# Gathers of u and v in turn, with single-buffer releases and early row numbers

## The reference

```python
cand = (v1[..., :, None] + v2[..., None, :]).reshape(bsz, seq, PEER_HEADS, PEER_TOPK * PEER_TOPK)
sc, ci = lax.top_k(cand, PEER_TOPK)
experts = (jnp.take_along_axis(i1, ci // PEER_TOPK, axis=-1) * PEER_NKEYS
           + jnp.take_along_axis(i2, ci % PEER_TOPK, axis=-1))
gates = jax.nn.softmax(sc, axis=-1)

def peer_block(args):
    hb, eb, gb = args
    u_sel = jnp.take(peer_u, eb, axis=0)
    z = jnp.einsum('td,tkd->tk', hb, u_sel)
    act = jax.nn.gelu(z, approximate=False) * gb
    return jnp.einsum('tk,tkd->td', act, jnp.take(peer_v, eb, axis=0))
```

## Time and profile before

| | |
|---|---|
| Time, median of 3 runs | 1563.23 us (1555.8 to 1563.44) |
| Profiled execution: span from first to last instruction | 1523.7 us; the time around the span was not recorded for it |
| PE, DVE, ACT, POOL busy | 1222.4, 989.9, 438.1, 645.2 us |
| Gather queue (q0) | 268.47 MB, 47.5% of 16 engines' span |
| Mean granted TensorE clock | 0.888 of 2.4 GHz |

### The profile page before, as it was taken

The page is one execution under the profiler, slowest core; times in us unless marked ns, Lnnn a source line. Parts: engine busy times, 40 slices in busy tenths (PEclk is TensorE's granted clock), DMA queues, the critical chain, the costliest instruction groups (busy, mean ns, idle before and its releaser), DMA issues.

```text
span 1523.7 us, 15861 instructions
## 1 busy us (share of the span) xinstructions
PE 1222.4 (80%) x5450; PEld 813.5 (53%) x5450; DVE 989.9 (65%) x1812; ACT 438.1 (29%) x853; POOL 645.2 (42%) x641
## 2 busy tenths in 40 slices
PE   6997898998888576675788768667667988799998
PEld 2983778566563222232344323223225977599986
DVE  6699879575555656756677555675446666478773
ACT  1564312122122112121131211212115452365651
POOL 4164203007564777767776777677750020000000
PEclk9998799999998887888999778788878999799999
DMA  9354031438998999999999999999986423355540
GB/s 355 134 193 140 27 111 56 166 111 313 356 385 316 351 352 340 355 354 358 368 338 335 358 345 357 339 366 368 345 290 234 157 93 111 124 166 166 175 165 28
DMA packets 139764, 380.97 MB, mean 250 GB/s; under 512 B 10707, under 2 KB 37742, under 8 KB 139706
## 3 DMA queue, kind: packets, MB, share of 16 engines
q0 software_dynamic: 73728, 268.47, 47.5%
q1 hardware_dynamic: 64656, 108.87, 20.7%
q10 hardware_dynamic: 1322, 2.85, 0.6%
HBM read 379.10 MB, written 1.05 MB: 249 GB/s over the span
## 4 chain that ended last, share of the span: by engine, by line
PE 56%; POOL 13%; DVE 13%; issue 8%; DMA 6%; ACT 3%; SPq 0%; POOLq 0%; DVEq 0%; ACTq 0%
PE banks L1048 20%; POOL arena L655 7%; PE banks L757 7%; PE banks L759 7%; PE banks L758 7%; POOL arena L647 6%; DMA arena<-in_peer_u,arena 4%; PE banks L1016 3%; DVE arena L1912 2%; DVE weight_ring L1836 2%; PE banks L701 2%; DMA weight_ring<-in_cond_w 1%; PE banks L997 1%; PE banks L730 1%; ACT arena L1540 1%
## 5 line engine op out<-in xcount | busy, mean ns | idle before, releaser
L1048 PE MATMUL banks<-arena 128*128 128x512 f32 x1012 | 508.9, 667 | 206.3 <-ACT arena L1540 182.3
L1048 PEld LDWEIGHTS banks<-arena 128*128 128x128 f32 x1012 | 214.8, 216 | 497.7 <-issue 286.9
L2169 DVE SCALAR_TENSOR_TENSOR arena<-arena 128x1024 f32<-128x1024 f32 x256 | 312.5, 1226 | 237.6 <-DMA arena<-in_peer_u,arena 231.8
L655 POOL DMA_INDIRECT arena<-in_peer_v,arena x256 | 271.2, 1059 | 142.1 <-issue 73.1
L647 POOL DMA_INDIRECT arena<-in_peer_u,arena x256 | 271.2, 1059 | 96.8 <-issue 69.7
L759 PE MATMUL banks<-hi_h,low_slot 128*128 128x256 f32 (+2 forms) x600 | 172.5, 288 | 0.0
L1533 ACT ACTIVATE arena<-arena 128x8 f32<-128x8 f32 x32 | 6.7, 208 | 455.6 <-DVE arena L2169 455.6
L759 PEld LDWEIGHTS banks<-hi_h,low_slot 128*128 128x128 f32 (+2 forms) x600 | 114.0, 190 | 0.6
L757 PE MATMUL banks<-hi_h,hi_w 128*128 128x256 f32 (+1 forms) x352 | 101.3, 288 | 2.7 <-DVE lo_h L2270 2.7
L758 PE MATMUL banks<-lo_h,hi_w 128*128 128x256 f32 (+1 forms) x352 | 100.0, 284 | 0.0
L1540 ACT ACTIVATE arena<-ident,arena 128x128 f32<-128x128 f32 x256 | 78.2, 388 | 13.4 <-DVE arena L2173 12.9
(11 more groups left out here) (367 smaller groups left out, 2070.6 us busy)
## 6 DMA issues: line engine op xcount, KB each, us to landing
weight_ring<-in_cond_w SPq DMA_DIRECT2D x12, 2048.0 KB, 9.6
weight_ring<-in_w_in SPq DMA_DIRECT2D x11, 2048.0 KB, 8.2
weight_ring<-in_ffn_w_up SPq DMA_DIRECT2D x20, 1024.0 KB, 6.8
weight_ring<-in_ffn_w_down SPq DMA_DIRECT2D x5, 2048.0 KB, 7.7
weight_ring<-in_w_out SPq DMA_DIRECT2D x4, 2048.0 KB, 7.7
weight_ring<-in_peer_wq SPq DMA_DIRECT2D x4, 2048.0 KB, 12.6
arena<-in_peer_u,arena POOLq DMA_INDIRECT x256, 5.9
arena<-in_peer_v,arena POOLq DMA_INDIRECT x256, 6.1
```

What stands on the lines that cost most here:

```text
L655: g.indirect_dma_start(v_rows[:, j, :], None, A["peer_v"], bass.IndirectOffsetOnAxis(ap=stage[:, r, j:j + 1], axis=0)).then_inc(sem(f"v_in ...
L1048: last = mm(acc[i], diag[:, r, j, :], v_rows[:, j, i * 512:(i + 1) * 512], start=False, stop=False)
L2169: ins = v.scalar_tensor_tensor(out=u_rows[:, j, :], in0=u_rows[:, j, :], scalar=1.0, in1=h2[:, t, :], op0=ALU.mult, op1=ALU.mult, accum_ou ...
```

## The change

Releases by the buffer: PE adds one to `v_free` behind each buffer and not behind the eighth, and DVE adds one to `u_free` with each dot. ACT's waits are for the same events with the new counts. POOL copies the 16 row numbers of a head at once, into one of three places of `stage`, in the first round of the head before, behind v gather 6. The gathers of u and v alternate: u of the next round, v of this round, each behind its own release. There is no loop; all 512 gathers are written out.

```diff
-            def gather(n):
-                for r in range(2):
...
-                    for j in range(8):
-                        g.indirect_dma_start(u_rows[:, j, :], None, A["peer_u"],
...
+            def copy_rows(n):
+
+                pool.wait_ge(sem("experts_ready"), n + 1)
+                g.tensor_copy(stage[:, n % 3, :], experts[:, n * TOPK:(n + 1) * TOPK]).then_inc(sem("staged"), 1)
+
+            rounds = 2 * (LAST + 1)
...
+            def gather_u(rnd, j):
+
+                if rnd:
+                    pool.wait_ge(sem("u_free"), (rnd - 1) * 8 + j + 1)
+                g.indirect_dma_start(u_rows[:, j, :], None, A["peer_u"], row_of(rnd, j)).then_inc(sem(f"u_in_{j}"), 16)
...
+                if rnd:
+                    pool.wait_ge(sem("v_free"), (rnd - 1) * 8 + j + 1)
...
+            copy_rows(0)
+            pool.wait_ge(sem("staged"), 1)
+            for j in range(8):
+                gather_u(0, j)
+
+            for rnd in range(rounds):
+                for j in range(8):
+                    if rnd + 1 < rounds:
+                        if rnd % 2 and j == 0:
+                            pool.wait_ge(sem("staged"), (rnd + 1) // 2 + 1)
+                        gather_u(rnd + 1, j)
+                    gather_v(rnd, j)
+                    if rnd % 2 == 0 and j == 6 and rnd // 2 < LAST:
+                        copy_rows(rnd // 2 + 1)
@@ sum_v (PE)
-                    last.then_inc(sem("v_free"), 1)
+                        last.then_inc(sem("v_free"), 1)
@@ activate (ACT)
-                    act.wait_ge(sem("u_free"), n * 2 + (r + 1))
+                    act.wait_ge(sem("u_free"), n * 16 + 8 * (r + 1))
...
-                        act.wait_ge(sem("v_free"), n * 2 + (r - 1))
+                        act.wait_ge(sem("v_free"), n * 16 + 8 * (r - 1))
@@ dots (DVE)
-                        ins.then_inc(sem("u_free" if j == 7 else "u_part"), 1)
+                        ins.then_inc(sem("u_free"), 1)
```

More of the change, by code:

```diff
@@ L373, in block_kernel @@
         aw = at(SM + 272, 2, 8)
-        stage = at(SM + 288, 16).bitcast(U32).rearrange("p (a b) -> p a b", b=8)
+        stage = at(SM + 864, 3 * TOPK).bitcast(U32).rearrange("p (a b) -> p a b", b=TOPK)
         experts = at(SM + 304, (NT * PEER_H + 1) * TOPK).bitcast(U32)
@@ L631, in _ @@
                            sem("off_ready"))
-            def gather(n):
-                for r in range(2):
-                    pool.wait_ge(sem("experts_ready"), n + 1)
-                    g.tensor_copy(stage[:, r, :], experts[:, bass.ds(n * TOPK + 8 * r, 8)]).then_inc(sem("staged"), 1)
-                    pool.wait_ge(sem("staged"), n * 2 + (r + 1))
-                    g.nop(nofuse=True)
-                    first = isinstance(n, int) and n * 2 + r == 0
-                    if not first:
-                        pool.wait_ge(sem("u_free"), n * 2 + r)
-                        g.nop(nofuse=True)
-                    for j in range(8):
-                        g.indirect_dma_start(u_rows[:, j, :], None, A["peer_u"],
-                                             bass.IndirectOffsetOnAxis(ap=stage[:, r, j:j + 1], axis=0)
-                                             ).then_inc(sem(f"u_in_{j}"), 16)
-                    if not first:
-                        pool.wait_ge(sem("v_free"), n * 2 + r)
-                        g.nop(nofuse=True)
-                    for j in range(8):
-                        g.indirect_dma_start(v_rows[:, j, :], None, A["peer_v"],
-                                             bass.IndirectOffsetOnAxis(ap=stage[:, r, j:j + 1], axis=0)
-                                             ).then_inc(sem(f"v_in_{j}"), 16)
@@ L659, in _, with row_of @@
-            gather(0)
-            gather(1)
-            for t in range(NT):
-                with pool.Fori(max(2, t * PEER_H), (t + 1) * PEER_H) as n:
-                    gather(n)
+            def copy_rows(n):
+                pool.wait_ge(sem("experts_ready"), n + 1)
+                g.tensor_copy(stage[:, n % 3, :], experts[:, n * TOPK:(n + 1) * TOPK]).then_inc(sem("staged"), 1)
+            rounds = 2 * (LAST + 1)
+            def row_of(rnd, j):
+                return bass.IndirectOffsetOnAxis(ap=stage[:, rnd // 2 % 3, 8 * (rnd % 2) + j:8 * (rnd % 2) + j + 1], axis=0)
@@ new lines, in gather_u, with gather_v @@
+            def gather_u(rnd, j):
+                if rnd:
+                    pool.wait_ge(sem("u_free"), (rnd - 1) * 8 + j + 1)
+                g.indirect_dma_start(u_rows[:, j, :], None, A["peer_u"], row_of(rnd, j)).then_inc(sem(f"u_in_{j}"), 16)
+            def gather_v(rnd, j):
+                if rnd:
+                    pool.wait_ge(sem("v_free"), (rnd - 1) * 8 + j + 1)
+                g.indirect_dma_start(v_rows[:, j, :], None, A["peer_v"], row_of(rnd, j)).then_inc(sem(f"v_in_{j}"), 16)
```

## The result

The changed kernel took 1600.99 us (median of 4 runs, 1589.13 to 1604.01), the kernel before 1559.51 on the same chip (1553.23 to 1563.44): ratio 1.0277 [1.0196, 1.0358]. I had forecast 1530. The runs behind it fell on several chips, and that matters here: on most of them before takes 1531 to 1532 us, and there the change is 0.995 to 0.996. On one more, where before takes 1555.6, it is 1.019. I call the two kinds the fast and the slow chips; each chip was measured in one session, so its own speed and what ran beside it then can't be told apart. Each run is compared with before on its own chip. The interval of the first result lies wholly above 1, so the change was slower there, by about 2 to 3.6%.

The account below looks back on a forecast made before the run. POOL, with 38 + 22 us of waits in the 619.5 us middle stretch, and DMA at 0.95 were the near limits. Middle 29, start 2 and end 2 us less: span 1523.7 to 1491, plus 39.5 gives 1530 us; range 1513 to 1562.

Parts of the forecast that it names:

- Part 4: POOL's new pace in the middle stretch: 391 us of gathers, 52 of lengthening beside dots, 127 gaps, 3 copies: 573 us.
- The rule that I weighed: Two-input DVE instructions and GpSimd SBUF reads exclude each other: up to 1.23 us a dot; judged too large against the trace.
- Part 3: Row numbers copied once a head on POOL: 21.7 us of waits and 2.7 of copies go; slack 1 to 3 us.
- The start: 344.8 to 487.7 us: sum 0 ends 4 to 5 us later, then regained; net 2 us less.
- Part 1: Single-buffer releases: each gather waits for its own dot or sum; no instruction added on DVE and PE, nothing lost on ACT.
- Part 2: POOL's u and v in turn: slack 15 us for v, 5 for u; POOL's 37.9 us of waits for PE go.
- Part 5: DMA in the middle stretch: the same packets take 590 us at a full share, which can be had.
- Part 6: POOL's unrolled program: at most a few hundred KB more instructions to load, beside 218 MB of rows; costs nothing.
- The wait's price: Rival: a wait on each POOL gather costs time, deciding above 0.11 us each; slower, chance 0.11.
- DMA's limit: Rival: DMA gives no more than now, 353 GB/s in the middle, about 1560 us; chance 0.13, of which 0.09 no change.
- PE's clock: Rival: PE's short steps keep it at 1.2 GHz, 27.9 us a round, +106 us; chance 0.04.
- The copy stall: Rival: with later landings POOL stops at the copy, losing 20 of the 29 us, about 1550; chance 0.11.

Follow-up runs that it names:

- e4: The changed kernel on a fast chip, against the kernel before: 1524.99 us, ratio 0.9959.
- the first run: The changed kernel's first measurement and profile, on a slow chip, against the kernel before: 1600.99 us, ratio 1.0277.
- e8: The changed kernel with dots that read only the u buffer (one input, output not the reference's), fast chip: 1449.04 us, 0.9459 of before.
- e17: e2 with dots that read only the u buffer (one input), on a fast chip: 1434.51 us, 0.9375 of before.
- e0: The kernel before, unchanged, profiled again on a fast chip: 1530.16 us.
- e2: Kernel before with single-buffer releases, waits on the gathers themselves, loop written out, old order and copies kept; fast chip: 1478.53 us, 0.9665 of before.
- e3: e2 plus early row numbers, one copy of 16 a head behind v gather 6 of the odd round; fast chip: 1480.96 us, 0.9675 of before.
- e14: The changed kernel again, on a slow chip, against the kernel before: 1582.69 us, ratio 1.0191.
- e7: e3 with eight u of the next round, then eight v of this one, copy where first needed; fast chip: 1495.79 us, 0.9773 of before.
- e12: e2 with dots that read only the u buffer (one input), on a slow chip: 1522.55 us, 0.9793 of before.
- e13: e7 with dots that read only the u buffer (one input), on a slow chip: 1544.12 us, 0.9937 of before.

## Why the prediction was wrong, step by step

- **Part 4, the dots' hold-up, is the step that failed on every chip.** I took the 48 us of before and scaled them with DVE's share of POOL's time, to 52. In e4 the same stretch has 479.2 - 413 x 0.94 = 91 us. That alone is 39 of the some 50 us by which POOL there misses its 573 us; the copy wait of 7.5 us is most of the rest, and gaps and copies are the remainder. The hold-up depends on how dots and gathers fall together, not only on how much. Of the gathers that have 0.7 us or more beside dots, the mean is 1.27 us in before (156 of 512) and 1.51 in the changed kernel (153 in the first run, 50 of them over 1.9; 144 in e4). That the hold-up as a whole is the larger part of the loss is shown by e8 and e17.
- **Which dots cost more** can be counted, if a gather's time over 0.94 us is put down to the dots that it overlaps. One kind are eight dots back to back behind a pick, when the u buffers have already landed (885 to 894 us in the first run: one each 1.145 us, beside gathers of 1.99). They come with the single releases and not with the turn: dots under 1.18 us apart are 24 of 256 in e0, 111 and 119 in e2 and e3, 129 in e4, and in the last three they cost 0.36 to 0.42 us each, 40, 50 and 53 us in all. The other kind is the turn's. In e3 the dots of the other rounds follow landings at the gathers' own pace, 1.18 to 1.4 us apart (124 of them), and cost 0.11 us each, 13 us in all. In e4 they stand over 2.2 us apart (107), and cost 0.36 each, 39 us in all. This is 26 of the 31 us by which e4's gathers are longer than e3's. Why a dot by itself costs a gather more than one in step with the gathers, the runs don't show.
- **The rule that I weighed**, the page "SBUF — State Buffer" of the Trainium skill (Who interferes with whom), is right that a DVE instruction with one SBUF input does not contend (0.94 us beside dots of 1.21). For two inputs, a whole exclusion of up to 1.23 us a dot is still more than the 1.05 us over 0.94 of the worst gathers and the 0.57 of the mean.
- **Part 3, the copy.** I named its slack of 1 to 3 us as the smallest, gave the stall 20 us and a chance of 0.11. On a fast chip it does hold in the middle: e4's copies for heads 3 to 9 and 11 to 15 wait for nothing. It failed in two other places. One is the start, below. The other is that a slack of 1 to 3 us has to carry each lateness of the pick, and on the slow chips seven and eight of 15 picks were 2 to 9 us late: 39 (e14) to 61 us (first run) of copy waits more than in e4, out of 47 and 71 us by which the stage is longer. Outside the stage the three profiles agree (739.7, 736.8 and 741.1 us).
- **"The wait behind each copy for its own result"**, 21.7 us, did go, but I had its cause wrong: most of it goes in e2 too, where the copies stay (0.27 us and not 0.83).
- **The start.** I had 2 us less. On a fast chip the first copy went as I had it: it waits 8.93 us and goes at 383.93, and v(0, 7) goes at 385.55 (e4). What I had wrong is the landing. With u between them, the v rows of round 0 land 4 us apart and not 2 (v(0, 6) at 390.74, where before has 377.56), so v(0, 7) lands at 394.84 and not at 391, and sum 0 ends 9 us later than before, not 4 to 5. I had no second stop either, and the copy for head 2 waits 13.88 us. In the first run the two wait 17.25 (it goes at 392.09) and 14.45. The step that failed: I moved v(0, 7) and forgot who stands behind PE. ACT works in order; its gelu of a head's first round stands behind evictions of queries and scores, which PE makes only behind the sums, and the sums wait for v, now a round late. At the tile's change, ACT and DVE of the first run:

```profile
872.60 0.60 ACT L1309 ACTIVATE mem_kv<-banks 128x512 f32<-128x512 f32 x1 [33.19 <-remote]
```

```profile
873.46 0.17 DVE L2179 TENSOR_TENSOR arena<-arena 128x8 f32<-128x8 f32 x1 [16.64 <-ACT arena L1539]
```

  The weights of heads 0, 1 and 9 come 18.2, 18.3 and 16.6 us behind their last dot (9.9, 16.6 and 10.0 in e4; 9.6, 4.5 and 3.4 before), and with them the pick, the row numbers and the copy, in front of which POOL stands. Part of the rise comes without the lag (10.3, 8.3 and 5.6 in e3; 10.5, 16.4 and 19.4 in e7, with it). e7 against e3 prices the lag, with the copy in front of its first use, at 0.9773 against 0.9675.
- **Part 1 was right**, and is where most of the gain is: with single releases the waits of v gathers for PE fall from 69.7 (e0) to 22.7 us (e2).
- **Part 2 was right on v** (POOL's waits for PE go) **and right in the middle on u.** The 5 us of slack hold on the fast chips (13.7 us of u waits in the whole stage of e4, ordinary gaps among them); in the first run 24.6 us came with the long picks.
- **Part 5, DMA's pace**, was right as a limit: 398 to 401 GB/s at 1.00 to 1.01 (e8, e17), 375 at 0.98 (e2). The change never got there.
- **Part 6** held: e2 is unrolled as well, and gains.
- **The chances** add up a little otherwise than I wrote: same 0.11 and slower 0.15.
- **The end**: I had 2 us less, because PE would have one or two sums left when the last row lands. It has five, as before: one burst of 11.87 us behind a landing in the first run, 10.55 in e4.
- **The base.** "39.5 us over the span" was a misreading. A profiled execution lies 1.8 us over its span (1604.01 and 1602.2). The profile of before, at 1523.7, is by its length one of a fast chip (1521 to 1540 us there, 1541 to 1564 on the slow ones), and the median beside it is of a slow one. On its own ground the forecast was 33 us less, about 1498 on a fast chip; 1524 to 1525 were measured, 7 less.
- **The rivals.** The wait's price: wrong, gaps are 0.30 on gathers with a wait. DMA's limit: wrong. PE's clock: wrong, the granted clock is 0.94, nearer the level of 2.4 GHz than before, with sums in steps of 1.98 us. The copy stall: right in kind, and too cheap; on the slow chips it is the largest term of what the changed kernel loses there, and by reason of late picks, not of landings.

What stays open: why DVE pauses inside picks on some chips, or in some sessions, and whether before has some of it there (no trace of it was taken on one); whether e2 keeps its full lead there. With one-input dots (e12) it leads e13, 0.979 against 0.994, but it has lost most of what it gained on a fast chip (0.9375), to waits for PE.

## What to carry to other kernels

Release buffers one by one, but leave the order alone until a trace shows that it must change: here single releases in the old order, with the waits put on the gathers themselves, are worth 3.3% on a fast chip, and the new order gave back all but 0.4 to 0.5% of it. On slow chips the changed kernel was 1.9 to 2.8% slower than before, and e2 was not tried there. An instruction that waits in an in-order queue of issues needs a slack larger than the variation of what it waits for, and a consumer moved a round later moves every in-order queue behind it. Where descriptor work on POOL sets the pace, count which DVE instructions with two on-chip inputs run beside it, and how closely: one input instead of two was worth 44 to 75 us in the kernels with single releases.

## What the runs showed of the hardware

- A gather of 128 rows costs POOL 0.94 us and a gap of 0.30, with or without a satisfied wait, and 0.94 beside a DVE instruction with one input (e8); beside one with two inputs up to 1.99.
- A gather that waits for the copy just in front of it starts 0.27 us behind it when the wait stands on the gather (e2), 0.83 when it stands on a `nop` (before).
- One core's gathers reach 398 to 401 GB/s over 572 us, and the DMA engines 412 in shorter stretches (e13, 588 to 590 us).
- Chips, or sessions on them, differ. The same kernel takes 1525 or 1583 to 1601 us, and the difference lies in pauses of 0.8 to 4.3 us between instructions of DVE (and some of POOL) that wait for nothing named; in the two such stretches shown the DMA engines' share is 1.02 to 1.04.
